# Branch weights in a place of their own, mix weights moved ahead in the load queue, and held copies moved ahead of merged tiles, in a hybrid decoder trunk on one core

## The reference

```python
proj = x @ w_in + b_in                      # x: 512 x 1024
qa, ka, va, qb, kb, vb, qc, kc, vc, fc, gates = jnp.split(proj, ...)
o_a, o_b, o_c = three attention branches    # 256, 512 and 256 columns
g = sigmoid(gates).reshape(B, S, 3, 1024)
merged = g[:, :, 0] * (o_a @ w_a) + g[:, :, 1] * (o_b @ w_b) + g[:, :, 2] * (o_c @ w_c)
h = merged @ w_out
x = LN(alpha * x + h)                       # ln1
x = LN(alpha * x + MemoryCrossAttn(x, mem)) # ln2
x = LN(alpha * x + SwiGLU(x))               # ln3
```

## Time and profile before

| | us |
|---|---|
| median of 3 runs | 867.27 (866.64 to 869.36) |
| the profiled execution's own time | 867.53 |
| its span, first to last instruction | 865.8 |
| mean granted TensorE clock | 0.995 of full |
| PE busy | 849.8 (98%) |
| PE weight loads busy | 752.3 (87%) |
| DVE busy | 615.4 (71%) |
| ACT busy | 410.8 (47%) |
| POOL busy | 97.1 (11%) |

### The profile page before, as it was taken

How to read it: one execution, slowest core, us unless ns; L and a number is a source line. 1 busy time by engine, 2 the same in 40 slices (tenths; PEclk the granted TensorE clock), 3 DMA queues, 4 the chain that set the end, 5 groups by cost and what they waited for, 6 DMA issues and landing times.

```text
span 865.8 us, 14104 instructions
## 1 busy us (share of the span) xinstructions
PE 849.8 (98%) x5418; PEld 752.3 (87%) x5418; DVE 615.4 (71%) x1116; ACT 410.8 (47%) x847; POOL 97.1 (11%) x112
## 2 busy tenths in 40 slices
PE   9999999999999999999899999999999999999996
PEld 9988898877678999998689979899999999888785
DVE  5444357778566969795567689689888898877944
ACT  5121176248643545564324645365565556424511
POOL 4100000262301101110000000101121111000000
PEclk9999999999999999999999999999999999999998
DMA  9525622230013141415622311223332233651101
GB/s 305 152 97 146 123 98 89 83 98 2 1 48 100 49 146 50 146 56 188 243 98 83 112 50 50 97 76 120 99 98 99 98 100 120 252 211 49 49 25 73
DMA packets 73119, 90.47 MB, mean 104 GB/s; under 512 B 3458, under 2 KB 63638, under 8 KB 73054
## 3 DMA queue, kind: packets, MB, share of 16 engines
q1 hardware_dynamic: 72670, 89.15, 31.0%
q0 software_dynamic: 384, 0.43, 0.3%
HBM read 87.05 MB, written 2.52 MB: 103 GB/s over the span
## 4 chain that ended last, share of the span: by engine, by line
PE 47%; DVE 2%; issue 1%; DMA 1%; ACT 1%; DVEq 0%; POOLq 0%; POOL 0%; ACTq 0%
PE ps L3407 7%; PE ps L3409 7%; PE ps L3408 7%; PE ps L2798 6%; PE ps L2799 6%; PE ps L2800 6%; PE ps L3465 1%; PE ps L3466 1%; PE ps L3467 1%; DMA raw<-in_w_mix_out 1%; PE ps L2835 1%; PE ps L2924 1%; PE ps L3001 0%; PE ps L2961 0%; PE ps L3350 0%
## 5 line engine op out<-in xcount | busy, mean ns | idle before, releaser
L1283 ACT CAST w_hi<-raw 128x1024 fp32r<-128x1024 f32 (+1 forms) x54 | 55.7, 1034 | 129.4 <-PE ps L2800 107.5
L1863 DVE TENSOR_TENSOR w_lo<-raw,w_hi 128x1024 fp32r<-128x1024 f32 (+1 forms) x54 | 65.2, 1209 | 51.9 <-ACT w_hi L1283 51.8
L2798 PE MATMUL ps<-xt_hi,w_hi 128*128 128x512 f32 (+1 forms) x256 | 99.4, 388 | 0.0
L2800 PE MATMUL ps<-xt_lo,w_hi 128*128 128x512 f32 (+1 forms) x256 | 98.8, 386 | 0.0
L2799 PE MATMUL ps<-xt_hi,w_lo 128*128 128x512 f32 (+1 forms) x256 | 98.8, 386 | 0.0
L3407 PE MATMUL ps<-xt_hi,w_hi 128*128 128x256 f32 x288 | 81.6, 283 | 0.0
L3408 PE MATMUL ps<-xt_hi,w_lo 128*128 128x256 f32 x288 | 81.5, 283 | 0.0
L3409 PE MATMUL ps<-xt_lo,w_hi 128*128 128x256 f32 x288 | 81.5, 283 | 0.0
L3407 PE MATMUL ps<-s_hi,w_hi 128*128 128x256 f32 x216 | 61.1, 283 | 0.0
L3408 PE MATMUL ps<-s_hi,w_lo 128*128 128x256 f32 x216 | 61.1, 283 | 0.0
L3409 PE MATMUL ps<-s_lo,w_hi 128*128 128x256 f32 x216 | 61.1, 283 | 0.0
(11 more groups left out here) (430 smaller groups left out, 2426.9 us busy)
## 6 DMA issues: line engine op xcount, KB each, us to landing
raw<-in_w_ffn_in SPq DMA_DIRECT2D x36, 512.0 KB, 4.3
raw<-in_w_in SPq DMA_DIRECT2D x15, 1024.0 KB, 4.8
raw<-in_w_in SPq DMA_DIRECT2D x19, 512.0 KB, 4.3
raw<-in_w_ffn_out SPq DMA_DIRECT2D x7, 1024.0 KB, 4.9
raw<-in_w_mix_out SPq DMA_DIRECT2D x4, 1024.0 KB, 5.4
raw<-in_w_ffn_in SPq DMA_DIRECT2D x4, 1024.0 KB, 5.0
out_w<-in_w_ffn_out SPq DMA_DIRECT2D x4, 1024.0 KB, 9.0
raw<-in_w_branch_b SPq DMA_DIRECT2D x4, 512.0 KB, 4.0
```

The costliest lines, as they stand in the source:

```text
L1283: act.copy(hi, src).then_inc(hi_done, 1)
L1863: dve.tensor_tensor(lo, src, f32(hi), ALU.subtract).then_inc(lo_done, 1)
L2798: pe.matmul(dst, a_hi, b_hi, start=start, stop=False, skip_group_check=reopened)
L2800: return pe.matmul(dst, a_hi, b_lo, start=False, stop=stop, skip_group_check=reopened)
```

## The change

1. In the rounds the branch weights are no longer loaded into `raw[1]` but into the first half of `resid` (`branch_w`), and a block earlier: their three loads are issued ahead of the two loads of the round's third block (n = 2, 5, 8). The nine blocks then alternate strictly between `raw[0]` and `raw[1]`, and each waits for P3 of the block before the last. `GATE_HALVES` and `loads_before` count the loads accordingly.
2. The chunk CM+1 of the mix weights goes into `raw[1]` as soon as P3 of block 7 has been split; the first rows of `x` can be loaded only once the last branch weights have been split, and CM+2 and CM+3 stand ahead of the second rows of `x` and of ln1's two vectors.
3. On ACT `gate_u3` stands ahead of `merged_round` in a round's first block, and at the end of a block instead of the beginning of the next. On DVE the rest for P4 stands ahead of the two `merge_add`, and in the last tile the rest of PM+1 stands ahead of the third `merge_times`.

```diff
@@ -188,7 +188,7 @@
 GATE_OP = {key: m for m, key in enumerate(gate_products_in_order())}
 N_GATE_OPS = len(GATE_OP)
 N_GATE_BLOCK = 3 * (N_PAIR - 1)
-GATE_HALVES = (2 * (N_PAIR - 1), N_PAIR - 1)
+GATE_HALVES = ((N_GATE_BLOCK + 1) // 2, N_GATE_BLOCK // 2)
 
 
 def out_op(kind, k):
@@ -775,6 +775,8 @@
         X_12 = xs_b[:, :, :]
         GS1, GS2, GS3, GS4 = X_22, X_11, X_21, X_12
 
+        branch_w = resid[:, 0:2, :].rearrange("p t (k c) -> p (t k) c", k=4)
+
         def gate_sum(j, part):
 
             if j == 4:
@@ -794,15 +796,14 @@
 
         def gate_quarter(n, row, col):
 
-            k8 = raw[n % 3 % 2][:, :].rearrange("p (k c) -> p k c", k=KT)
+            k8 = raw[n % 2][:, :].rearrange("p (k c) -> p k c", k=KT)
             return k8[:, 4 * row:4 * row + 4, P * col:P * col + P]
 
         def gate_right(kind, n):
 
             if kind in ("K0", "K4"):
-                k8 = raw[1][:, :].rearrange("p (k c) -> p k c", k=KT)
                 k0 = 0 if kind == "K0" else 4
-                return k8[:, k0:k0 + 4, P * (n % 2):P * (n % 2) + P]
+                return branch_w[:, k0:k0 + 4, P * (n % 2):P * (n % 2) + P]
             if kind == "P5":
                 return g_t1[:, :, :]
             if kind in ("P6", "P4"):
@@ -811,7 +812,7 @@
 
         def loads_before(n):
 
-            return n // 3 + 1 if n % 3 == 1 else 2 * (n // 3) + n % 3 // 2 + 1
+            return n // 2 + 1
 
         GATE_A, GATE_B, GATE_C = (4, 7), (5, 0), (6, 1)
 
@@ -1040,38 +1041,42 @@
                 else:
                     for w, (k0, k1) in zip(w_br, ((0, 2), (2, 6), (6, 8))):
                         sp.dma_start(k8[:, k0:k1, :], w[:, :, 0:256]).then_inc(raw_in[1], 16)
+
+            def branch_weights(i):
+
+                if i > 1:
+                    sp.wait_ge(g_lo, GATE_OP["K4", 2 * i - 1] + 1)
+                for w, (k0, k1) in zip(w_br, ((0, 2), (2, 6), (6, 8))):
+                    sp.dma_start(branch_w[:, k0:k1, :], w[:, :, i * 256:(i + 1) * 256]).then_inc(branch_in, 16)
+
             for i in range(1, N_PAIR):
                 for n in range(3 * i - 3, 3 * i):
                     if n == 0:
                         sp.wait_ge(lo_done, PG + 6)
                     elif n == 1:
                         sp.wait_ge(lo_done, PG + 8)
-                    elif n % 3 == 0:
-                        sp.wait_ge(g_lo, GATE_OP["P3", n - 1] + 1)
-                    elif n % 3 == 1:
-                        sp.wait_ge(g_lo, GATE_OP["K4", 2 * i - 1] + 1)
                     else:
                         sp.wait_ge(g_lo, GATE_OP["P3", n - 2] + 1)
-                    k8 = raw[n % 3 % 2][:, :].rearrange("p (k c) -> p k c", k=KT)
+                    if n % 3 == 2:
+                        branch_weights(i)
+                    k8 = raw[n % 2][:, :].rearrange("p (k c) -> p k c", k=KT)
                     n0 = GATES + n % 3 * D + i * 256
-                    sp.dma_start(k8[:, 0:4, :], w_in[:, 0:4, n0:n0 + 256]).then_inc(gate_half[n % 3 % 2], 16)
-                    sp.dma_start(k8[:, 4:8, :], w_in[:, 4:8, n0:n0 + 256]).then_inc(gate_in[n % 3 % 2], 16)
-                sp.wait_ge(g_lo, GATE_OP["P3", 3 * i - 2] + 1)
-                k8 = raw[1][:, :].rearrange("p (k c) -> p k c", k=KT)
-                for w, (k0, k1) in zip(w_br, ((0, 2), (2, 6), (6, 8))):
-                    sp.dma_start(k8[:, k0:k1, :], w[:, :, i * 256:(i + 1) * 256]).then_inc(branch_in, 16)
+                    sp.dma_start(k8[:, 0:4, :], w_in[:, 0:4, n0:n0 + 256]).then_inc(gate_half[n % 2], 16)
+                    sp.dma_start(k8[:, 4:8, :], w_in[:, 4:8, n0:n0 + 256]).then_inc(gate_in[n % 2], 16)
             x_rows = A["x"][0].rearrange("(t p) n -> p t n", p=P)
+            sp.wait_ge(g_lo, GATE_OP["P3", N_GATE_BLOCK - 2] + 1)
+            load(CM + 1)
             sp.wait_ge(g_lo, GATE_OP["P3", N_GATE_BLOCK - 1] + 1)
             load(CM)
+            sp.wait_ge(g_lo, N_GATE_OPS)
             sp.dma_start(resid[:, 0:2, :], x_rows[:, 0:2, :]).then_inc(resid_in, 16)
-            sp.wait_ge(g_lo, N_GATE_OPS)
-            load(CM + 1)
-            load(CM + 2)
+            for c in range(CM + 2, CM + 4):
+                load(c)
             sp.wait_ge(g_prod, N_GATE_OPS)
             sp.dma_start(resid[:, 2:4, :], x_rows[:, 2:4, :]).then_inc(resid_in, 16)
             for i, w in enumerate(("ln1_g", "ln1_b")):
                 sp.dma_start(gb[:, i, :], A[w][0:1, :].to_broadcast([P, D])).then_inc(gb_in, 16)
-            for c in range(CM + 3, CF):
+            for c in range(CM + 4, CF):
                 load(c)
             sp.wait_ge(norm_done, TT)
             for i, w in enumerate(("ln2_g", "ln2_b")):
...
...
@@ -1505,14 +1510,14 @@
                 gate_round("P1", n + 1)
                 gate_u2(n)
                 gate_round("P4", n)
-                merged_round(2 * (n // 3) + 1)
                 sigmoid_left(n)
                 gate_round("P5", n + 1)
+                gate_u3(n)
+                merged_round(2 * (n // 3) + 1)
 
             def gate_inner(n, last):
 
                 i = n // 3 + 1
-                gate_u3(n - 1)
                 gate_round("P3", n - 1)
                 gate_seed(n)
                 gate_round("P6", n)
@@ -2243,9 +2249,9 @@
                 merge_times(i, 1, 2)
                 gate_t4(n)
                 gate_op_rest("P1", n + 1)
+                gate_op_rest("P4", n)
                 merge_add(i, 1, 1)
                 merge_add(i, 1, 2)
-                gate_op_rest("P4", n)
                 gate_op_rest("P5", n + 1)
                 merge_rest(2 * i + 1)
 
@@ -2333,9 +2339,9 @@
                 gate_tail(i)
             merge_times(N_PAIR - 1, 1, 0)
             merge_times(N_PAIR - 1, 1, 1)
+            rest_of(PM + 1)
             merge_times(N_PAIR - 1, 1, 2)
             merge_add(N_PAIR - 1, 1, 1)
-            rest_of(PM + 1)
             merge_add(N_PAIR - 1, 1, 2)
             merge_rest(KT - 1)
 
```

More of the change, by code:

```diff
@@ L1219, in gate_weight_sums @@
             def gate_weight_sums(n):
-                pool.wait_ge(gate_half[n % 3 % 2], 16 * loads_before(n))
+                pool.wait_ge(gate_half[n % 2], 16 * loads_before(n))
                 if n:
@@ L1443, in gate_round @@
                 elif kind == "P1":
-                    act.wait_ge(gate_half[n % 3 % 2], 16 * loads_before(n))
+                    act.wait_ge(gate_half[n % 2], 16 * loads_before(n))
                 elif kind in ("P2", "P3"):
-                    act.wait_ge(gate_in[n % 3 % 2], 16 * loads_before(n))
+                    act.wait_ge(gate_in[n % 2], 16 * loads_before(n))
                 else:
@@ L2212, in gate_t23 @@
                 dve.wait_ge(g_t1_done, n + 1)
-                dve.wait_ge(gate_in[n % 3 % 2], 16 * loads_before(n))
+                dve.wait_ge(gate_in[n % 2], 16 * loads_before(n))
                 if n:
```

## The result

| | before | after |
|---|---|---|
| median | 867.61 (866.64 to 869.36, 4 runs) | 877.43 (875.29 to 877.82, 4 runs) |
| ratio | | 1.0106 [1.0082, 1.0129] |
| the profiled execution | 867.53, span 865.8 | 877.12, span 875.2 |
| mean granted TensorE clock | 0.995 | 0.991 (0.988 to 0.994 over the runs) |

The account below looks back on a forecast made before the run. PE bounds the kernel, busy 849.8 of 865.8 us, so only its stops count. Rounds 2.7 slower (6.0 - 3.3) and mix product 2.6 faster (4.9 - 2.3) make 0.1 slower: 867.4 us, no change, range 864.0 to 872.0.

Parts of the forecast that it names:

- What goes in the rounds: Gate rounds: stops at P4 (1.22, 0.27, 0.27) and P7 (0.61, 0.95) vanish, 3.3 us off.
- The path of the new stop: Gate rounds: branch loads delay the third block's first half, its cast, then gate_u2's copy; P7 stops 6.0 us.
- 3D - 12.9: Gate rounds: sum of the three new P7 stops in us, 6.0 at the D chosen.
- D: Gate rounds: time from the load trigger to landing of the third block's first half, 3.4 us before the change.
- the estimated 0.7 us: Gate rounds: the trigger, P3's rest on DVE, comes 0.7 us earlier without the wait for gate_u3.
- I take D = 6.3: Gate rounds: chosen landing time of the first half, between 6.1 by bytes and 6.6; ends 4.8 and 8.
- the branch loads' own landing: Gate rounds: third branch load's landing at 5.2 to 6.7 us plus the half's 1.4 gives 6.6 to 8.1.
- The low clock: PE at 1.2 GHz behind a stop: 1.25 us lost before PM+6; up to 1.25 for each P7 stop of 3 to 4.
- The mix product: Mix product: 1.2 and 3.7 us off, 2.3 back at the transposes, 2.6 us faster.
- The new stop at the transposes: First transposes: PE waits for the layer norm behind PKX's splits, 2.3 us (1.4 to 3.4).
- the half is held up more: Gate rounds: D 7.7 or more, P7 stops 10.2, rounds 6.9 slower, possible clock drops: 871.5 to 874; chance 0.23.
- The first rival: Gate rounds: half not held up, D 4.8 to 5.4, rounds 0 to 1.8 faster: 863.3 to 864.5; chance 0.23.

Follow-up runs that it names:

- e1: Changed kernel with the third block's two gate loads issued ahead of the three branch loads in each round: 863.01 us, ratio to before 0.9951.
- e13: Changed kernel with two branch loads (b 512 KB, c 256 KB) ahead of the third block's halves, the branch a load behind them: 873.16 us, ratio to before 1.0075.
- e17: Changed kernel with only branch b's 512 KB ahead of the third block's halves, cut into four loads of 128 KB: 871.01 us, ratio to before 1.0054.
- e16: Changed kernel with only branch b's 512 KB ahead of the third block's halves, cut into two loads of 256 KB: 872.13 us, ratio to before 1.0068.
- e10: Changed kernel with the three branch loads issued between the two halves of the third block: 864.98 us, ratio to before 0.998.

## Why the prediction was wrong

By its own steps:

- **What goes in the rounds (3.3 us): right.** No P4 stop and no wait for branch weights are left; e1's rounds, which keep this gain without the new stops, take 123.8 us against 127.3 before, 3.5 less; undoing the copies' move alone brought 2.0 back (forecast for those 1.8).
- **The path of the new stop: right.** Loads ahead of the half, the cast late, `gate_u2` behind the cast, P7 waiting. And 3D - 12.9 held with its constant: the measured D sum to 23.0, which gives 10.1, and the stops were 9.8. So the constant, with the estimated 0.7 us by which the trigger comes earlier, held as a sum; no run measured the 0.7 by itself.
- **"I take D = 6.3": the step that failed.** It priced the megabyte ahead at 383 GB/s, the rate of a window in which one load ran. Measured were 7.3, 7.5 and 8.2. That is 4 us of stops more than forecast. The runs put in its place: bytes at that rate for one load ahead, and 1.1 to 1.6 us on top for two or more. The bytes priced the first of the half's 16 parts (6.0 us behind the trigger); ACT waits for the last (7.3, 7.5 and 8.1). The prediction had the evidence: the branch loads' own landing gave 6.6 to 8.1, and it set that aside as a slow transfer or two. That reading was literally right: in the third round before, 47 of the branch loads' 48 increments had come 5.2 us behind their trigger and the last at 6.7, with no window under 330 GB/s from 1.5 to 4 us behind it. To leave it out was the mistake, for a load has landed only with its last part. The rule of the Trainium skill that it named beside the sum ("DMA: Bandwidth & Descriptors", "Queues, rings and completion order"), that each DMA engine takes descriptors in ring order, agrees with these runs: with a load ahead the half came later in every round, 4.2 us or more behind the trigger against 3.8 or less. But order says nothing of the rate or of the spread.
- **The low clock: left out of the likeliest sum.** Stops of 3.4 and 3.5 us drew 4.1 us of it. The prediction had 1.25 for each drop as an upper bound, from the one stretch of the earlier trace rows; measured were 1.6 and 2.5. With the stops, the rounds are -3.3 + 9.8 + 4.1 = 10.6 by this account and 10.2 by the marks.
- **The mix product: right in kind, 2.2 us back against 2.6.** The stop of PM+1 went from 1.6 to 0.4, as forecast, and that before PM+6 went away whole, where 0.5 was to stay. The new stop at the transposes was 3.4, the upper end of 1.4 to 3.4, not 2.3; it was not followed by the low clock. What it waits for was forecast well: PKX's cast came 13.2 us behind the fourth chunk's issue (430.56 to 443.76; forecast 13.0) and the norm's end 8.7 behind that (8.7). PE was there 0.8 earlier than forecast, counted from that issue, and so waited longer.
- **The rivals.** The second, "the half is held up more", is what happened, with its condition (D over 7.1) and its 10.2 of stops. Its price of 871.5 to 874 was 3.4 too low: 1.6 of it is the low clock, taken at some 2.5 at most and measured 4.1; 1.4 is time lost ahead of the rounds (0.5) and behind the mix product (0.9), for which the forecast had nothing and no run shows a cause. With a chance of 0.23 it should have set the range's upper end; the range stopped inside it, at 872. The first rival's price does not follow from its own terms either: rounds 0 to 1.8 faster and 2.6 to 4.0 from the mix product give 861.5 to 864.7, not 863.3 to 864.5. It did not come true, so nothing hung on that.

## What to carry to other kernels

- In these runs a load put ahead of another under the same trigger cost the other its bytes, and 1.1 to 1.6 us more once several loads of 128 to 512 KB stood ahead. Look at what the load behind it feeds and how much slack that has; here it was 0.8 us, and issuing the urgent half first cost nothing.
- Take the price of queued loads from a row in which such loads were queued, not from the best rate of a window. A late last part that shows in two of three rounds is the price, for the reader waits for all 16.
- When a range rests on stops of some 3 us on TensorE, put the clock behind them into the sum.

## What was not expected of the hardware

- Cutting 512 KB in two loads of 256 KB (same rows, same buffer, same place in the queue) delayed the next load by 1.6 us and the kernel by 6.7 us (865.43 to 872.13), of which 5.1 are P7 stops (6.1 against 0.95) and 1.5 is the low clock behind the third of them. The load's first part was only 0.25 us later (4.67 against 4.42 behind the trigger); it is the last that came late.
- The length of a stop did not tell whether the clock falls. In the kernel with b and c ahead (e13) the granted clock fell to 0.50 behind a P7 stop that cost 2.15 us (round 3) and stayed at 1.00 behind one of 2.27 (round 2). It also fell behind 2.4 (e17, round 1) and 2.5 (e16, round 3), and did not behind 2.85 (346.19 in the changed kernel) and 3.4 (the transposes there). How long it stays low differs too: 1.6 us lost behind the changed kernel's first stop, 2.5 behind its third.
- Loads issued behind an urgent load slow it as well: D of the half rose from 3.7 to 4.2 to 4.5 when the branch loads, not the second half, came right behind it (e10).
